# Six of the twelve expert weight units of a step move from SP's DMA queue to GpSimd's

## The reference

```python
def add_expert(e, acc):
    h = xt @ w_gu[e]                                   # 1024 x 512
    a = jax.nn.silu(h[:, :D_EXPERT]) * h[:, D_EXPERT:]
    return acc + (a * gates_t[e][:, None]) @ w_down[e] # 256 x 1024
routed = lax.fori_loop(0, N_EXPERTS, add_expert, jnp.zeros_like(xt))
```

## Time and profile before

| | |
|---|---|
| median of 3 runs | 1847.18 us (1844.6, 1847.18, 1851.25) |
| profiled execution, its own time | 1845.16 us |
| its span | 1843.3 us |
| granted TensorE clock, mean | 0.969 |
| PE / DVE / ACT / POOL busy | 93 / 54 / 41 / 14 % of the span |
| 32 steps of experts | from about 220 to 880 us and from about 1135 to 1795 us |

### The profile page before, as it was taken

The page is one execution under the profiler, slowest core; times in us unless marked ns, Lnnn a source line. Parts: engine busy times, 40 slices in busy tenths (PEclk is TensorE's granted clock), DMA queues, the critical chain, the costliest instruction groups (busy, mean ns, idle before and its releaser), DMA issues.

```text
span 1843.3 us, 29568 instructions
## 1 busy us (share of the span) xinstructions
PE 1721.8 (93%) x10290; PEld 1311.6 (71%) x10290; DVE 1002.8 (54%) x1425; ACT 764.9 (41%) x1028; POOL 254.1 (14%) x180
## 2 busy tenths in 40 slices
PE   7988799999999999999889887999999999999996
PEld 6878677677677776777578685677677777777774
DVE  2774455555555555555437644555555555555554
ACT  4563333343444444443254722343444444443432
POOL 6653000000000000000065610000000000000000
PEclk9998899999999999999989888999999999999998
DMA  9422589989988898888663126899999898988883
GB/s 293 139 70 69 204 323 329 332 329 335 332 336 338 335 335 324 325 335 320 211 217 123 62 69 242 324 326 338 334 339 336 338 329 326 329 336 318 333 325 114
DMA packets 136699, 510.31 MB, mean 277 GB/s; under 512 B 11684, under 2 KB 51016, under 8 KB 103368
## 3 DMA queue, kind: packets, MB, share of 16 engines
q1 hardware_dynamic: 122896, 468.81, 69.0%
q0 software_dynamic: 9792, 35.66, 6.1%
q10 hardware_dynamic: 3960, 5.17, 0.9%
HBM read 506.19 MB, written 3.41 MB: 276 GB/s over the span
## 4 chain that ended last, share of the span: by engine, by line
PE 80%; issue 8%; DVE 4%; DMA 4%; ACT 2%; POOL 1%; DVEq 1%; SPq 0%; ACTq 0%; POOLq 0%
PE ps L994 11%; PE ps L689 9%; PE ps L968 9%; PE ps L890 9%; PE ps L867 7%; PE ps L904 6%; PE ps L868 6%; PE ps L869 6%; PE ps L1035 6%; PE ps L1009 4%; PE ps L897 2%; DMA raw<-in_w_exp_down_dram 2%; DVE o_lo L1600 1%; ACT o_hi L1309 1%; DMA xg_b<-x_by_token,token_b 1%
## 5 line engine op out<-in xcount | busy, mean ns | idle before, releaser
L1572 DVE TENSOR_TENSOR raw_r<-raw,w_hi 128x2048 fp32r<-128x2048 f32 x192 | 440.0, 2292 | 393.2 <-ACT w_hi L1257 393.0
L1257 ACT CAST w_hi<-raw 128x2048 fp32r<-128x2048 f32 x192 | 365.9, 1906 | 283.3 <-DMA raw<-in_w_exp_down_dram 174.7
L867 PE MATMUL ps<-x_hi,w_hi 128*128 128x256 f32 x1088 | 311.4, 286 | 1.8 <-DVE x_lo L1497 1.8
L868 PE MATMUL ps<-x_lo,w_hi 128*128 128x256 f32 x1088 | 306.9, 282 | 0.0
L869 PE MATMUL ps<-x_hi,raw_r 128*128 128x256 f32 x1088 | 306.3, 282 | 0.0
L994 PE MATMUL ps<-raw,xc 128*64 128x512 f32 x1024 | 233.8, 598 | 0.0
L867 PEld LDWEIGHTS ps<-x_hi,w_hi 128*128 128x128 f32 x1088 | 206.6, 190 | 31.4 <-issue 30.1
L868 PEld LDWEIGHTS ps<-x_lo,w_hi 128*128 128x128 f32 x1088 | 207.9, 191 | 1.5
L652 POOL DMA_INDIRECT xg_b<-x_by_token,token_b x32 | 32.6, 1019 | 1264.8 <-DVE token_c L1552 1264.8
L869 PEld LDWEIGHTS ps<-x_hi,raw_r 128*128 128x128 f32 x1088 | 206.7, 190 | 0.0
L994 PEld LDWEIGHTS ps<-raw,xc 128*64 128x64 f32 x1024 | 67.8, 136 | 119.4 <-issue 115.0
(11 more groups left out here) (295 smaller groups left out, 3009.5 us busy)
## 6 DMA issues: line engine op xcount, KB each, us to landing
raw<-in_w_exp_gu_dram SPq DMA_DIRECT2D x256, 1024.0 KB, 6.7
raw<-in_w_exp_down_dram SPq DMA_DIRECT2D x128, 1024.0 KB, 7.1
raw<-in_w_in_dram SPq DMA_DIRECT2D x22, 1024.0 KB, 7.1
raw<-in_w_out_dram SPq DMA_DIRECT2D x8, 1024.0 KB, 5.1
row_b<-gates_by_rank SPq DMA_DIRECT2D x32, 256.0 KB, 5.6
row_c<-gates_by_rank SPq DMA_DIRECT2D x64, 128.0 KB, 5.3
raw<-in_w_sh_gu_dram SPq DMA_DIRECT2D x4, 1024.0 KB, 5.1
row_a<-gates_by_rank SPq DMA_DIRECT2D x32, 128.0 KB, 8.1
```

The source lines that it names most:

```text
L867: nc.tensor.matmul(o, h, x_hi[:, c, :], start=(first and i == 0), stop=False, skip_group_check=True)
L868: nc.tensor.matmul(o, h, x_lo[:, c, :], start=False, stop=False, skip_group_check=True)
L1257: nc.scalar.copy(w_hi[CAST[j] % 3][:], raw[:, j % RING, 0:UNIT_F]).then_inc(hi_done, 1)
L1572: nc.vector.tensor_tensor(raw_r[:, s, 0:UNIT_F], raw[:, s, 0:UNIT_F], w_hi[CAST[j] % 3][:], ALU.subtract)\
```

## The change

GpSimd loads the pair's six units (C10, C20, C11, C21, C1D, C2D) in every step. SP keeps B0, B1, A0, A1, BD, AD and the row broadcasts. The pair's units get a semaphore each (`pair_loaded`). Each queue has its own waits on `unit_used`, and no unit's slot, size or release changes. No instruction of TensorE, ScalarE or VectorE changes, apart from the semaphore on which the pair's matmuls wait.

```diff
@@ -87,7 +87,6 @@
-    PER_SLOT = [fills(NEXT + s) + 2 * NIT for s in range(RING)]
...
+    BY_SP = [[j for j in range(U12) if j % RING == s and CLASS[j] < 2] for s in range(RING)]
+    PER_SLOT = [fills(NEXT + s) + len(BY_SP[s]) * NIT for s in range(RING)]
...
+        pair_loaded = {j: layer_sem(f"pair_loaded{j}", 16 * NIT) for j in range(U12) if CLASS[j] >= 2}
...
+            if CLASS[j] >= 2:
+                return pair_loaded[j], done(layer, pair_loaded[j], it * 16 + 16)
             s = j % RING
-            return raw_loaded[s], layer * (16 * PER_SLOT[s]) + it * 32 + 16 * (fills(NEXT + s) + j // RING + 1)
+            return raw_loaded[s], layer * (16 * PER_SLOT[s]) + it * (16 * len(BY_SP[s])) \
+                + 16 * (fills(NEXT + s) + BY_SP[s].index(j) + 1)
...
+        def ranked_expert(eng, it, c):
+
+            return eng.value_load(order[0:1, bass.ds(it * 4 + c, 1)], min_val=0, max_val=NE - 1)
+
+        def load_piece(eng, layer, j, e):
+
+            eng.dma_start(piece_slot(j % RING, PIECE[j]), expert_sources(w_exp_gu[layer, e], w_exp_down[layer, e])[PIECE[j]])\
+                .then_inc(raw_loaded[j % RING] if CLASS[j] < 2 else pair_loaded[j], 16)
...
-                    e = expert[CLASS[j]]
-                    sp.dma_start(piece_slot(j % RING, PIECE[j]), expert_sources(w_exp_gu[layer, e], w_exp_down[layer, e])[PIECE[j]])\
-                        .then_inc(raw_loaded[j % RING], 16)
...
                 sp.wait_ge(order_ready, done(layer, order_ready, 1))
                 sp.sem_inc(order_turn, 1)
-                expert = {}
-                for j in range(RING):
-                    if CLASS[j] not in expert:
-                        expert[CLASS[j]] = ranked_expert(0, CLASS[j])
-                    if j < 3:
-                        read(sp, layer, NEXT + j - RING)
-                    else:
-                        sp.wait_ge(unit_used, done(layer, unit_used, j - 2))
-                    load_piece(0, j, expert)
-                    if j == A0:
-                        sp.wait_ge(ranked_stored, done(layer, ranked_stored, 16))
-                        load_rows_bc(0)
-                        load_row_a(0)
-
-                def second_half(it, more):
-
-                    expert = {}
-                    for j in range(RING, U12):
-                        if CLASS[j] not in expert:
-                            expert[CLASS[j]] = ranked_expert(it, CLASS[j])
+                e_b, e_a = ranked_expert(sp, 0, 1), ranked_expert(sp, 0, 0)
+                for j, e in ((B0, e_b), (B1, e_b), (A0, e_a)):
+                    read(sp, layer, NEXT + j - RING)
+                    load_piece(sp, layer, j, e)
+                sp.wait_ge(ranked_stored, done(layer, ranked_stored, 16))
+                load_rows_bc(0)
+                load_row_a(0)
+                sp.wait_ge(unit_used, done(layer, unit_used, A1 - 2))
+                load_piece(sp, layer, A1, e_a)
+
+                def down_units(it):
+
+                    for j in (BD, AD):
+                        e = ranked_expert(sp, it, CLASS[j])
                         sp.wait_ge(unit_used, used(layer, it, j - RING))
-                        load_piece(it, j, expert)
-                        if j == C11 and more:
-                            sp.wait_ge(place_c_ready, done(layer, place_c_ready, it + 1))
-                            sp.sem_inc(order_turn, 1)
-                            load_rows_bc(it + 1)
+                        load_piece(sp, layer, j, e)
 
                 with sp.Fori(0, NIT - 1) as it:
-                    second_half(it, True)
-                    expert = {}
-                    for j in range(RING):
-                        if CLASS[j] not in expert:
-                            expert[CLASS[j]] = ranked_expert(it + 1, CLASS[j])
+                    sp.wait_ge(place_c_ready, done(layer, place_c_ready, it + 1))
+                    sp.sem_inc(order_turn, 1)
+                    load_rows_bc(it + 1)
+                    down_units(it)
+                    e_b, e_a = ranked_expert(sp, it + 1, 1), ranked_expert(sp, it + 1, 0)
+                    for j, e in ((B0, e_b), (B1, e_b), (A0, e_a)):
                         sp.wait_ge(unit_used, used(layer, it, j + RING))
-                        load_piece(it + 1, j, expert)
-                        if j == A0:
-                            sp.wait_ge(a_ready, done(layer, a_ready, it + 2))
-                            sp.sem_inc(order_turn, 1)
-                            load_row_a(it + 1)
-                second_half(NIT - 1, False)
+                        load_piece(sp, layer, j, e)
+                    sp.wait_ge(a_ready, done(layer, a_ready, it + 2))
+                    sp.sem_inc(order_turn, 1)
+                    load_row_a(it + 1)
+                    sp.wait_ge(unit_used, used(layer, it, A1 + RING))
+                    load_piece(sp, layer, A1, e_a)
+                down_units(NIT - 1)
...
-                with pool.Fori(0, NIT) as it:
+
+                def gather_rows(it):
+
                     pool.wait_ge(token_ready, done(layer, token_ready, it + 1))
                     pool.sem_inc(pool_turn, 1)
                     pool.indirect_dma_start(xg_b[:], None, x_rows, bass.IndirectOffsetOnAxis(ap=token_b[:, 0:1], axis=0))\
                         .then_inc(xg_b_loaded, 16)
                     pool.indirect_dma_start(xg_c[:], None, x_rows, bass.IndirectOffsetOnAxis(ap=token_c[:, 0:1], axis=0))\
                         .then_inc(xg_c_loaded, 16)
+
+                def pair_units(it, units, e, after):
+
+                    for j, c in zip(units, e):
+                        pool.wait_ge(unit_used, used(layer, it, j - RING) if after is None else done(layer, unit_used, j - after))
+                        pool.sem_inc(pool_turn, 1)
+                        load_piece(pool, layer, j, c)
+
+                def pair_of(it):
+
+                    return ranked_expert(pool, it, 2), ranked_expert(pool, it, 3)
+
+                pool.wait_ge(order_ready, done(layer, order_ready, 1))
+                pool.sem_inc(pool_turn, 1)
+                pair_units(0, (C10, C20), pair_of(0), 2)
+                gather_rows(0)
+                with pool.Fori(0, NIT - 1) as it:
+                    e = pair_of(it)
+                    pair_units(it, (C11, C21), e, None)
+                    gather_rows(it + 1)
+                    pair_units(it, (C1D, C2D), e, None)
+                    pair_units(it + 1, (C10, C20), pair_of(it + 1), None)
+                e = pair_of(NIT - 1)
+                pair_units(NIT - 1, (C11, C21), e, None)
+                pair_units(NIT - 1, (C1D, C2D), e, None)
```

More of the change, by code:

```diff
@@ L511, in _ @@
                 sp.dma_start(ln_b[:], ln2_b[layer].partition_broadcast(P)).then_inc(ln2_loaded, 16)
-                def ranked_expert(it, c):
-                    return sp.value_load(order[0:1, bass.ds(it * 4 + c, 1)], min_val=0, max_val=NE - 1)
-                def load_piece(it, j, expert):
-                    e = expert[CLASS[j]]
-                    sp.dma_start(piece_slot(j % RING, PIECE[j]), expert_sources(w_exp_gu[layer, e], w_exp_down[layer, e])[PIECE[j]])\
-                        .then_inc(raw_loaded[j % RING], 16)
                 def load_row_a(it):
```

## The result

The changed kernel takes 1890.74 us (median of 4 runs, 1883.21 to 1894.76), the kernel before 1847.85 us beside it; the ratio is 1.0227, with an interval of 1.0187 to 1.0267. That is slower by 43 us, and the prediction of 1848.6 us was wrong, and so was its range. The profiled execution took 1888.13 us, with a span of 1886.3 us, against 1843.3 before: 43.0 us more.

The account below looks back on a forecast made before the run. The prediction took TensorE to bound the steps (42.66 of 43.10 us busy), with the DMA engines 89% busy. Its terms, 0 + 3.4 - 2.0 = +1.4 us, gave a median of 1848.6 us, range 1839 to 1866.

Parts of the forecast that it names:

- The quiet step: Each of the 30 steps of 43.07 us: late units keep within their margins, so the change costs 0.
- AD's margin: In a quiet step, AD has 0.65 us to spare before TensorE needs a_c; claimed not to be late, cost 0.
- C2D's: In a step, 5 us are left for C2D even with the longest gather landing, 8.4 us; cost 0.
- one of the signs on my list: In the steps, TensorE waiting at L1035 or L994 for the pair's DMAs would show the prediction wrong.
- B0 and B1: Next step's units: same bytes until B1 is in, so same landing; margin 1.25 us, cost 0 at equal rates.
- Equal shares of the engines: Transfers on both queues reckoned by bytes over the 430 GB/s that the DMA engines move when saturated.
- The start: Before each layer's first step: rows 4.9 us later, gather 3.2 us quicker, +1.7 a layer, +3.4 in both.
- The first step: First step of each layer: C21 issued some 3 us earlier shrinks the backlog ahead of AD; gain 2.0 us.
- Rival 1: GpSimd's queue moves bytes more slowly, B1's margin is exceeded in every step; at 50% slower 1885 us; chance 0.16.
- Rival 3: GpSimd's issues held up by VectorE's splits; before the first steps +9.2 us in all, 1858 us; chance 0.05.
- Rival 2: Layer starts cost more: rows 4.9 us later, no quicker gather, +9.8, no first-step gain, 1857 us; chance 0.11.
- `o_lo` moves behind B1's split: VectorE's order late in a step; o_lo coming after that split would show the prediction wrong.

Follow-up runs that it names:

- e1: Changed kernel with C11 and C21 put back on SP's queue at their old places around the row broadcasts; 1853.97 us, ratio 1.0041 to the kernel before.
- e6: Changed kernel, all six units on GpSimd, the loop's row broadcasts cut to 16 partitions (output not the reference's); 1850.18 us, ratio 1.0009 to the kernel before.
- e8: No unit on GpSimd, as in the kernel before, but ScalarE issues the loop's row broadcasts on its own queue; 1863.63 us, ratio 1.0088.
- e14: Changed kernel with only C10 and C20 on GpSimd's queue, the other ten units on SP's; 1852.25 us, ratio 1.0022 to the kernel before.
- e11: No unit on GpSimd, all twelve on SP, the loop's row broadcasts cut to 16 partitions (output not the reference's); 1844.70 us, ratio 0.9979 to the kernel before.
- e7: Changed kernel with only C11 and C21 on GpSimd's queue, the other ten units on SP's; 1866.16 us, ratio 1.0094 to the kernel before.
- e10: Changed kernel with only C1D and C2D on GpSimd's queue, the other ten units on SP's; 1849.34 us, ratio 1.0006 to the kernel before.
- e13: Changed kernel with C11, C21, C1D and C2D on GpSimd's queue, C10 and C20 back on SP's; 1880.03 us, ratio 1.0179 to the kernel before.
- e3: Changed kernel, but in each step GpSimd issues C11 only when the next step's row_c has landed; 2060.33 us, ratio 1.1146 to the kernel before.

## Why the prediction was wrong

**The quiet step, "Cost 0, thirty times": this is where it failed.** It cost 34.5 us. I checked AD, B0, B1 and C2D one by one. AD's margin held: its cast in the step above has no wait for a DMA. C2D's held but for two steps of layer 1, in which TensorE waited 4.0 us for a down unit, one of the signs on my list. I left out two things. The row broadcasts of the loop stand between C11 and C21 on SP's queue, and VectorE needs them in every step; and BD stands behind C21, with a margin that I never worked out. It was small: BD's split ended at 587.21 + 2.29 = 589.50 us, `gated` started at 589.70; `a_lo` was ready at 592.55, and TensorE came for it at 593.18 (its first L1009 of the step). That is 0.20 + 0.63 = 0.83 us. BD came 1.44 us later after the change, and 1.44 - 0.83 = 0.61 us is what TensorE waited. The sentence "it only changes who stands behind whom" was true, and the question that should have followed, who was protected by standing there, I asked only for the last units. e1 and e6 show the cause from two sides, the units and the rows' bytes: in both BD's cast is back at 10.1 us, and so is the step at 43.1.

**B0 and B1, "the same bytes, so its landing is the same".** It wasn't: B0's cast moved by 2.3 us against `a_b`, over the margin of 1.25. The bytes are the same, but they come later in the step: C1D stands behind the gathers on GpSimd's queue, these wait for the rows, and its issue at 560.22 is 13.1 us behind `a_b`, where SP's issues of AD and C1D had ended at 10.1.

**Equal shares of the engines.** I reckoned with bytes over 430 GB/s. In 2 us in which rows move, the engines were 102% busy and moved 273 GB/s; in one queue it was 330 GB/s, so 430 was too much there even before the change. The Trainium skill, "DMA: Bandwidth & Descriptors", section "Queues, rings and completion order", says that each DMA engine goes round the queues packet by packet. By that rule a broadcast of small packets beside units of large ones gets its turns but few bytes in each, and takes long for its size; for `row_c` the trace agrees (5.3 us in one line, 7.5 in two), for `row_b`, which is now issued ahead of C11, it does not show that (5.6 and 4.8). The same page's section "Issuing engines are not separate DMA queues" says that DMAs of all issuers share the same 16 engines and interleave; e8 agrees, where ScalarE's queue for the rows alone made the kernel 16 us slower, with the transfers late and not the issues. I had used neither.

**The start, +3.4 us.** It was 7.1 in the trace, within my bounds of -7 to +9.8. C10 and C20 alone cost less by the medians, 4.1 us by the ratio of e14, and the starts of e6 are 3.9 us longer than those of e11; with C10 and C20 on SP (e7, e10, e13) the starts are about those of before. The chain after shows the terms:

```profile
199.05 8.05 DMA gates_by_rank<-ranked
...
208.09 7.25 DMA row_c<-gates_by_rank
...
219.96 5.41 DMA xg_c<-x_by_token,token_c
```

Against the earlier trace rows the store is 1.75 us and `row_c` 3.70 us later, 5.45 in all where I took 4.9. The gather was to give back 3.2 us, and here the size was off. From the first gather's issue to TensorE's start on the tokens it takes 217.43 to 225.42, 8.0 us, as before (209.60 to 217.71). Only the way on from there is 1.7 us shorter, as `xg_b` is already turned when `xg_c` lands. 5.45 - 0.1 - 1.7 = 3.6 a layer.

**The first step, -2.0 us.** First steps took 44.45 and 44.51 us, 0.3 us less in all than before, though the median step grew by 1.1.

**Rival 1**, a slower queue: refuted by 0.146 against 0.150% a MB, and by e10, where 64 MB on it cost nothing that can be measured. **Rival 3**, issues held up by VectorE: an issue took 0.53 to 0.57 us for gate and up units and 0.70 to 0.80 for down units over the whole run, in which VectorE made 192 splits; refuted. **Rival 2** named +9.8 us at the start, where the trace has 7.1, but that place held a sixth of the whole. The sign "`o_lo` moves behind B1's split" was on my list of what would refute the forecast, and the step above shows it; I had no rival that led to it, and none with BD.

## What to carry to other kernels

When transfers are dealt to a second queue, don't only ask whether the moved ones still arrive in time: list every transfer that stays and was behind or between them, small and large, and give each its margin in the step. Here one queue kept C11, the rows, C21 and BD in an order that met every margin; on two queues `row_c` and C21 shared the engines and both landed late, and BD behind them. If the margins are under 1 us, move only transfers whose time in the step is free of such neighbours, as C1D and C2D here.

## What the runs showed of the hardware

- The broadcasts of a step were issued at about the same time with the 1 MB units around them on the same queue or on another. The two of `row_c` landed in 5.3 us in the median on the one queue and in 7.5 (up to 11.4) with the units on the other; that of `row_b` landed in 5.6 us behind C11 on the one queue and in 4.8 us when it was issued ahead of C11. Cut to 16 partitions `row_b` landed in 1.7 us in the median.
- In e3 a 1 MB unit on SP's queue (BD) was issued 1.5 us behind a 1 MB unit on GpSimd's (C11) and beside a second one (C21), and landed 11.0 us after its issue, where 5.0 us is what it took without them. In the trace's packet records of that step BD's first bytes move only 2.8 us after its issue (before the change 1.0 us), when 121 of C11's 128 pieces of 8 KB had started. From there on the two queues moved side by side: in the next 5.9 us the other 135 pieces of C11 and C21 started, 1.1 MB, and 231 pieces of 4 KB of SP's queue, 0.9 MB. So the unit that came first mostly went first, and the later ones shared. Sharing alone, after twice its own bytes, would have BD through in an estimated 2.1 / 0.43 = 4.9 us at the rate of the earlier trace rows and the fixed part of a transfer.
- GpSimd issued a plain 1 MB load in 0.53 to 0.80 us, faster than a gather (0.94 to 2.23 us).
